# Float32r parts instead of bfloat16 parts for the one-hot gathering and spreading of a mixture-of-experts kernel

## The reference

```python
def hier_moe(x, w_group, w_expert, w_gate, w_up, w_down):
    ...
    rows = xpad[row_tok].reshape(n_blocks, MOE_BLOCK, d)

    def expert_block(args):
        xb, e = args
        h = jax.nn.silu(xb @ w_gate[e]) * (xb @ w_up[e])
        return h @ w_down[e]

    yb = lax.map(expert_block, (rows, block_expert)).reshape(P, d)
    out = jax.ops.segment_sum(yb * row_w[:, None], row_tok, num_segments=T + 1)[:T]
    return out.reshape(b, s, d)
```

## Time and profile before

| | |
|---|---|
| median of 3 runs | 1808.4 us (1807.47 to 1808.51) |
| profiled execution, span | 1806.1 us |
| PE busy | 1786.0 us (99%) |
| DVE, ACT, POOL busy | 721.9, 448.2, 70.9 us |
| moved by DMA | 527.41 MB, of it 516.70 MB through SP's queue |
| float32 gate and up products, L876 | 1856 recorded |
| gathering in bfloat16, L810 | 672 recorded, 78.0 us |
| spreading in bfloat16, L928 | 270 recorded, 69.4 us |

### The profile page before, as it was taken

How to read it: one execution, slowest core, us unless ns; L and a number is a source line. 1 busy time by engine, 2 the same in 40 slices (tenths; PEclk the granted TensorE clock), 3 DMA queues, 4 the chain that set the end, 5 groups by cost and what they waited for, 6 DMA issues and landing times.

```text
span 1806.1 us, 21261 instructions
## 1 busy us (share of the span) xinstructions
PE 1786.0 (99%) x8612; PEld 984.0 (54%) x8647; DVE 721.9 (40%) x1667; ACT 448.2 (25%) x958; POOL 70.9 (4%) x66
## 2 busy tenths in 40 slices
PE   9999999999999999999999999999999999999999
PEld 8888754443443333455444344343366767568874
DVE  3566754212221213035421221221345566234675
ACT  2332312111111100133210111110134534217780
POOL 0000000000000000000000000000011110001110
PEclk9999999999999999999999999999999999999999
DMA  9723569999999999708899999999942332041520
GB/s 389 305 83 139 193 254 410 420 427 428 426 428 429 427 427 425 309 1 349 357 425 428 428 427 427 428 427 427 425 162 94 140 123 110 7 181 47 236 91 23
DMA packets 41828, 527.41 MB, mean 292 GB/s; under 512 B 4800, under 2 KB 5472, under 8 KB 8576
## 3 DMA queue, kind: packets, MB, share of 16 engines
q1 hardware_dynamic: 39200, 516.70, 68.7%
q10 hardware_dynamic: 2528, 9.31, 1.3%
HBM read 524.91 MB, written 1.08 MB: 291 GB/s over the span
## 4 chain that ended last, share of the span: by engine, by line
PE 88%; DMA 9%; DVE 2%; SPq 1%; ACT 0%; issue 0%; POOL 0%; DVEq 0%; ACTq 0%
PE ps L212 32%; PE ps L876 20%; PE ps L911 10%; DMA ring<-in_wu 6%; PE ps L810 4%; PE ps L928 3%; PE ps L715 2%; DMA ring<-in_w_lat 2%; PE ps L1702 2%; PE ps L1670 2%; PE ps L1234 1%; PE ps L679 1%; PE ps L1717 1%; PE ps L883 1%; PE ps L1446 1%; PE ps L1459 1%
## 5 line engine op out<-in xcount | busy, mean ns | idle before, releaser
L876 PE MATMUL ps<-ring,work 128*64 128x512 f32 x1856 | 409.1, 593 | 6.0 <-DMA ring<-in_wu 5.7
L212 PE MATMUL ps<-xl,ring 128*128 128x256 f32 (+3 forms) x1344 | 291.5, 375 | 0.4 <-DMA ring<-in_w_x 0.4
L876 PEld LDWEIGHTS ps<-ring,work 128*64 128x64 f32 x1856 | 131.6, 137 | 270.7 <-issue 251.2
L212 PEld LDWEIGHTS ps<-xl,ring 128*128 128x128 f32 x1344 | 243.7, 190 | 39.5 <-issue 2.5
L911 PE MATMUL ps<-ring,work 128*64 128x512 f32 x816 | 181.5, 594 | 0.1
L212 PE MATMUL ps<-ring,xl 128*128 128x256 f32 (+1 forms) x576 | 176.0, 463 | 0.2 <-ACT xl L1787 0.2
L2647 DVE TENSOR_TENSOR work<-work,ps 128x512 f32<-128x512 f32 x32 | 22.0, 688 | 361.4 <-PE ps L876 341.7
L212 PEld LDWEIGHTS ps<-ring,xl 128*128 128x128 f32 x576 | 108.3, 190 | 59.3 <-issue 49.9
L911 PEld LDWEIGHTS ps<-ring,work 128*64 128x64 f32 x816 | 56.2, 137 | 100.3 <-issue 98.7
L3178 POOL TENSOR_TENSOR small<-small,halves 128x1 f32<-128x1 f32 (+4 forms) x42 | 45.7, 1087 | 1545.7 <-DVE small L2449 936.6
L2608 DVE SCALAR_TENSOR_TENSOR work<-ps,small,big 128x512 f32<-128x512 f32 x60 | 45.0, 750 | 135.8 <-ACT big L1918 135.8
(11 more groups left out here) (476 smaller groups left out, 1958.9 us busy)
## 6 DMA issues: line engine op xcount, KB each, us to landing
ring<-in_wg SPq DMA_DIRECT2D x62, 2048.0 KB, 20.6
ring<-in_wu SPq DMA_DIRECT2D x52, 2048.0 KB, 21.7
ring<-in_wd SPq DMA_DIRECT2D x48, 2048.0 KB, 22.0
xl<-in_wd SPq DMA_DIRECT2D x10, 2048.0 KB, 23.5
xl<-in_wu SPq DMA_DIRECT2D x9, 2048.0 KB, 19.1
ring<-in_w_odd SPq DMA_DIRECT2D x8, 2048.0 KB, 7.4
ring<-in_w_xz SPq DMA_DIRECT2D x7, 2048.0 KB, 22.9
ring<-in_w_qkv SPq DMA_DIRECT2D x6, 2048.0 KB, 34.3
```

Source lines behind the costliest of these rows:

```text
L212: i = e.matmul(bout, lhs(k), rhs(k), start=start and k == ks[0], stop=stop and k == ks[-1])
L876: last = e.matmul(b[64 * j:64 * j + 64, :], x[:, 4 * a + k, 64 * j:64 * j + 64], w[k // 2][:, 2 * (k % 2) + j, :], start=a + k == 0, stop= ...
```

## The change

The 0/1 matrices, the parts of h and the parts of the result rows are kept as float32r, another four-byte type of the language, and a value is split into two such parts, not three. So

- a gathering is 16 products of 256 columns, not 24, and a spreading 8 of 512 columns, not 12;
- DVE makes one further part of each half of the result rows, not two, and the parts of h are one copy (ACT) and one subtraction (DVE) a layer;
- the slot product is 2 products for all 128 rows, not 4 for 64 each, and its table loses the third part of the weights;
- the parts of the result rows, `yr`, take 1 MB, and it is the 1 MB of `lnb` (`yr` is named at the same place as `lnb`, `hr` at that of `big`, the matrices at that of `work`).

So `lnb` is no longer free during the mixture. `BESIDE` is gone: chunk `md` of pair 8 is loaded whole through the ring, and ACT's DMA is no longer there. The norm's parameters can be loaded only once the spreading of pair 14 has read `yr`, so SP waits for that.

```diff
-BESIDE, TAIL = (8, 0), (15, 1)
+TAIL = (15, 1)
...
+        with nc.sbuf_tensor("yr", [128, 2, 1024], F32R) as yr:
+            pass
         lnb = sb("lnb", [128, 2, 1024])
+        with nc.sbuf_tensor("hr", [128, 2, 2, 1024], F32R) as hr:
+            pass
         big = sb("big", [128, 16 * 272])
+        with nc.sbuf_tensor("sr", [128, 2, 2, 256], F32R) as sr, nc.sbuf_tensor("swt", [128, 2, 256], F32R) as swt, \
+                nc.sbuf_tensor("tab", [128, 2, 32, 4], F32R) as tab:
+            pass
...
                         o, c = b[:, k * 256:(k + 1) * 256], (4 * (s % 2) + 2 * i + k) * 128
-                        for t, j in each(range(2), range(3)):
-                            last = e.matmul(o, hb[:, j, t, c:c + 128], Sb[:, s // 2 % 2, t, :],
-                                            start=t + j == 0, stop=t + j == 3)
+                        for t, j in each(range(2), range(2)):
+                            last = e.matmul(o, hr[:, j, t, c:c + 128], sr[:, s // 2 % 2, t, :],
+                                            start=t + j == 0, stop=t + j == 2)
...
-                if (p, n) == BESIDE:
-                    blocks[0:2] = [beside[:, 0:1024], beside[:, 1024:2048]]
-                    landed = {0: (ln_in, 16 * (3 * l + 2)), 2: landed[0]}
-                elif (p, n) == TAIL:
+                if (p, n) == TAIL:
...
-                for j in range(3):
-                    last = e.matmul(macc[t][n][:, :], SWT[:, p % 2, t * 128:(t + 1) * 128], ypart(j, n),
+                for j in range(2):
+                    last = e.matmul(macc[t][n][:, :], swt[:, p % 2, t * 128:(t + 1) * 128], yr[:, j, n * 512:(n + 1) * 512],
                                     start=p + j == 0, stop=False)
...
             e.activation(s4[:, :, 4], s4[:, :, 3], ACT.Exp).then_inc(*e_exp.up(l))
-            e.wait_ge(*ln_out(f"m{l}", 1, 1))
-            e.dma_start(beside, A["wd"][l, BESIDE[0], BESIDE[1]][:, 0:2048]).then_inc(ln_in, 16)
...
-            if n:
-                e.wait_ge(*ys0(l, p))
-            e.scalar_tensor_tensor(out=hs, in0=row_b[n][:, :], scalar=wsl[:, p % 2:p % 2 + 1], in1=ypart(0, n),
-                                   op0=ALU.mult, op1=ALU.subtract).then_inc(*vs.up())
-            e.wait_ge(*vs())
-            e.tensor_copy(ypart(1, n), hs).then_inc(*vs.up())
-            e.wait_ge(*vs())
-            e.tensor_tensor(ypart(2, n), hs, ypart(1, n), ALU.subtract).then_inc(*(ys1 if n else ys0).up(l, p))
+            part = slice(n * 512, (n + 1) * 512)
+            e.scalar_tensor_tensor(out=yr[:, 1, part], in0=row_b[n][:, :], scalar=wsl[:, p % 2:p % 2 + 1],
+                                   in1=yr[:, 0, part].bitcast(F32), op0=ALU.mult, op1=ALU.subtract
+                                   ).then_inc(*(ys1 if n else ys0).up(l, p))
...
-                        elif name == "md" and (p, a) == BESIDE:
-                            e.wait_ge(*ring.before(name, l, p, a))
-                            sync_part(e, w[l, p, a], slice(2048, 4096), ring(name, l, p, a)[0], name, l, p, a)
...
-            e.wait_ge(*dn_mm(l, *BESIDE))
+            e.wait_ge(*spr_mm(l, NE // 2 - 2))
             load_ln(e, 2 * l + 1)
```

More of the change, by code:

```diff
@@ L12 @@
 F32 = mybir.dt.float32
+F32R = mybir.dt.float32r
 BF16 = mybir.dt.bfloat16
@@ L470, in build, with rows_of @@
         m = Arena(work, 7680)
[L471 to L478, removed]
+        m(1792)
+        token, scaled = m(128).bitcast(BF16), m(128)
         xgT, sg, hs, hT = m(2, 8, 256), m(512), m(512), m(4, 128)
         xR = xgT[:, 1]
[L481 to L482 removed]
+        ys = area(big, 0, (1024,))
         mst = small[:, 696:700]
[L484 to L489, removed]
         aside = [big[:, 2048:4096], xgT[:, 1].rearrange("p k n -> p (k n)")]
[L492 removed]
+        def rows_of(s, t):
+            return sr[:, s // 2 % 2, t, 128 * (s % 2):128 * (s % 2) + 128]
         gx, hx, hTx = area(big, 2048, (512,)), area(big, 2560, (512,)), area(big, 3072, (4, 128))
@@ L819, in tensor_slots @@
                 e.wait_ge(*swt_in(l, 0))
-            for j, t in each(range(2), range(2)):
-                o, c = ps[0][64 * j:64 * j + 64, 0:4], 128 * (p % 2) + 64 * j
-                if p < 2:
-                    last = e.matmul(o, S[:, p, t, 64 * j:64 * j + 64], tabf[:, t, 2 * p + j, :], start=t == 0, stop=t == 1)
-                else:
-                    last = e.matmul(o, Sb[:, p // 2 % 2, t, c:c + 64], tab[:, t, 2 * p + j, :], start=t == 0, stop=t == 1)
+            for t in range(2):
+                last = e.matmul(ps[0][:, 0:8], rows_of(p, t), tab[:, t, 2 * p:2 * p + 2, :].rearrange("p e c -> p (e c)"),
+                                start=t == 0, stop=t == 1)
             last.then_inc(*slot_mm.up(l, p))
@@ L2591, in vector_slots @@
             i = p % 2
-            e.tensor_copy(slot[:, i], ps[0][:, 0:4]).then_inc(*vs.up())
+            for j in range(2):
+                r = slice(64 * j, 64 * j + 64)
+                e.tensor_copy(slot[r, i], ps[0][r, 4 * j:4 * j + 4]).then_inc(*vs.up())
             e.wait_ge(*vs())
-            e.tensor_reduce(wsl[:, i:i + 1], slot[:, i, 1:4], AXX, ALU.add).then_inc(*vs.up())
-            e.tensor_scalar(SWTf if p == NE // 2 - 1 else SWT[:, i], token, slot[:, i, 0:1], None, ALU.is_equal
+            e.tensor_reduce(wsl[:, i:i + 1], slot[:, i, 1:3], AXX, ALU.add).then_inc(*vs.up())
+            e.tensor_scalar(swt[:, i], token, slot[:, i, 0:1], None, ALU.is_equal
                             ).then_inc(*swt_in.up(l, p))
```

46 lines of the change are left out of this document (16 added, 30 removed).

## The result

| | median of its runs | lowest to highest |
|---|---|---|
| kernel before, beside the changed one | 1807.7 us (10 runs) | 1806.4 to 1808.5 |
| changed kernel | 1812.3 us (10 runs) | 1811.0 to 1813.4 |

The ratio is 1.0025, 95% interval 1.0016 to 1.0035: the changed kernel is 4.5 us slower. The forecast was +4.9 us, 1813.3. The profiled execution has a span of 1810.5 us, against 1806.1.

The account below looks back on a forecast made before the run. The prediction took the full DMA engines, through the landing of each mixture's last chunks, to bound the kernel. Its terms, +4.9 for the half chunk and four zeros, on 1808.4 gave 1813.3 us, range 1808 to 1820.

Parts of the forecast that it names:

- The bound: In the mixtures the DMA engines are full; 29.5 us a pair against PE's 26.57, so the last chunks' landing sets the end.
- Part 1: Pair 8's half chunk moves from a DMA hole into the full stretch: 1.049 MB, 2.46 us a layer, +4.9 us.
- landing isn't held back: Rival, chance 0.11: 427 GB/s throughout the stretch gives back 0.8 us a layer, 1811.7; no change from about 1.4.
- Part 2: PE in the mixture's middle: cheaper float32r products save 24.9 us a layer, but PE only waits for the landing, so nothing.
- The lower end: Gathering and spreading: float32r products cost the same as bfloat16, 0.212 and 0.109 us, a gain of 1.72 us a pair.
- the transposes' row: Four float32 transposes in 0.44 us, 0.11 for 128 columns, the nearest evidence for float32r products of 0.43 and 0.216 us.
- the middle price: Rival, chance 0.07: float32r products at 0.43 and 0.216 us, PE loses 25.3 us a layer, +43, 1852.
- the bound from the weight load: Gathering: float32 weight loads of 190 ns make sixteen products at least 3.04 us; without overlap a rival, +75, 1883, chance 0.03.
- Part 3: Behind the last up chunk: less spreading, but the path goes through DVE and ACT; 0, at most 0.4 us a layer.
- Part 4: SP's wait for pair 14's spreading before the norm's parameters: nothing, covered by 4 us of DMA work left.
- the sum: Five terms over the whole kernel: +4.9 + 0 + 0 + 0 + 0 on 1808.4, giving 1813.3 us.
- The signs: Profile after: first weight wait near 505 us, DMA at 427 GB/s, empty hole, layer 0's last up chunk at 697 us.

Follow-up runs that it names:

- kernel before with the lighter load: Kernel before, one half of every second chunk of pairs 3 to 14 not loaded in both layers (results wrong): 1797.8 us, ratio 0.9941.
- two kernels with the lighter load: Kernel before and changed kernel, each without one half of every second chunk of pairs 3 to 14 (results wrong): 1797.8 and 1761.0 us.

## Why the prediction was right, point by point

**The bound.** Right. The end of a mixture is the landing of its last up chunk, by four runs: the half chunk alone costs what the change costs, leaving it out gives 4.0 us back, three give 14.5, and 9 us lost by PE in the middle give and take nothing.

**Part 1, the half chunk, +2.46 a layer.** The mechanism was right, and the size too high in the changed kernel: 1.57 and 2.03 us, 3.6 for the two, not 4.9. For the half chunk by itself it was nearly right: the kernel before with this edit alone lost 1.95 and 2.68, 4.6 for the two, and one half chunk less in the changed kernel gained 2.94 in layer 0. Differences of up to 0.6 us in one landing say nothing. What part 1 left out is that with float32r parts the DMA engines' rate answers a little. Packets and MB from 280 to 690 us, before and then after:

```profile
DMA packets 12354, 174.74 MB, mean 426 GB/s; under 512 B 1367, under 2 KB 1367, under 8 KB 1367
```

```profile
DMA packets 12297, 175.03 MB, mean 427 GB/s; under 512 B 1357, under 2 KB 1357, under 8 KB 1357
```

The changed kernel moved 0.29 MB more in the same time, 0.7 us of work. The other kernels bear it out: 174.93 to 175.04 MB in the four more with float32r and no half chunk in the hole, 174.79 in the two more with bfloat16 parts. It was made up early: from 300 to 350 us the rate is 422 GB/s, before 418. This is the rival "landing isn't held back" at half its strength: it had to give back 1.4 us a layer to count. The hole before 280 us stayed nearly empty, as forecast (70 GB/s from 276 to 280 us, where the kernel before moves 276).

**Part 2, float32r.** The lower end was the right choice, but not exact. Its price of a bfloat16 spreading was misread: the chain has eleven of the twelve products, and the missing one is the "issue" piece ahead of them. The kernel before with the lighter load has all twelve:

```profile
476.81 0.16 issue
```

```profile
477.12 2.69 PE ps L928 x12
```

So a spreading took 2.70 us, 0.225 a product, not 2.54 and 0.212; the pair's 26.57 us hold it already. The float32r products cost 0.256 and 0.119 us, not 0.212 and 0.109. A pair falls by 26.57 - 25.26 = 1.31 us, not 1.72: 0.65 in the spreading, 0.71 in the gathering, the rest in the slot and down products. That is 18.4 us a layer by the two kernels with the lighter load, not 24.9. That the transposes' row does not stand for float32r was a choice, given as one with its chance, and it held: the middle price, 0.43 and 0.216, is out. So is the bound from the weight load: it is 190 ns in float32r, as feared, yet sixteen of them with their products take 1.91 us and not 3.04. The page's group of these loads has 55.1 us for 448, 0.123 each, so they overlap each other in the record, and here the mean of a weight load is no floor for the distance of products. Apart from the rate above, none of this reached the time, since all of it lies behind the transfers, as the prediction said.

**Part 3, nothing gained behind the last up chunk.** Right: from there to the down product it takes 702.05 - 696.21 = 5.84 us, before 700.47 - 694.64 = 5.83.

**Part 4, the new wait.** Right at nothing, ratio 1.0 in the run with it alone, but for a wrong reason. I said that the DMA engines have 4 us of work left when SP is released and don't run dry. They do run short: in the changed kernel they move 332 GB/s from 700 to 702 us and 270 from 702 to 704, where the kernel before moves 424 and 412, which is 1.1 us of work. It costs nothing because what comes late is not waited for: the parameters' load is issued at 701.87 us in layer 0, and the one in layer 1 lands 6.6 us after its issue. By that it is there at about 708.5, an estimate, and DVE wanted it at 710.56 even before.

**What the sum did not have.** The gap of 1.28 us behind the branch, +1.56 in the timeline and 0.9 to 1.8 by the times of the two kernels that have it not, and the wait of 0.60 us for the next stage's weights in layer 1, which was a wait of PE for something that doesn't move with PE's own lateness and went when PE came later. With part 1 too high by 1.3 us, the errors cancel: 3.6 + 1.56 - 0.7 = 4.5, against 4.9. That the total came nearer than its terms is luck; the bound and its price in bytes are not. The new gap is a part of the changed kernel's loss that has nothing to do with its idea: with it moved away, the changed kernel is at 1810.4 to 1810.6, still 3 us above the kernel before.

**The signs.** Of those I had named, the row x448, DMA at 427 to 428, the empty hole, and the last up chunk near 697 (696.21) came. The first wait for weights in layer 0 stands at 508.70 us and is short (0.38), the first long one (1.33) at 513.68; the forecast said near 505. The waits were 41.1 us in all, not 60, since the products were dearer than I took them to be. PE's busy time fell by 25.3 us, not 50: a pair saves 1.31 us, and the groups that wait are recorded longer.

## What to carry to other kernels

When DMA and PE are both near full, ask which one runs out of lead: a pair's bytes at the measured rate against a pair's PE time tells it before any change, and then only bytes and holes in the transfers count, however much PE work is saved. On-chip space that lets a transfer start in an otherwise empty hole is then worth its bytes over the full rate, and should not be paid for faster products that wait. A gap marked "issue" that comes without any change nearby may belong to the place of the code; move the code by some dozens of instructions before you explain it. Look at the granted clock behind such a gap, and at that of every execution: here executions with a mean clock of 0.999 were 2 to 3 us longer than others of the same kernel, half of what the change costs, where the clock fell at the end of a mixture.

## What the runs showed of the hardware that I had not expected

- A float32r product of 128 x 128 weights takes 0.256 us for 512 columns and 0.119 for 256, with a weight load of 190 ns; in bfloat16 it was 0.225, 0.109 and 98 ns (the first from the kernel before with the lighter load, the others from the earlier trace rows). Two float32r parts are cheaper than three bfloat16 parts, 3.96 us against 5.32 for a pair's gathering and spreading, by less than the count of products says. The Trainium skill, "TensorE: Matmul & The Clock Gate", Weight-path perf modes, keeps the fast weight load from FP32 and doesn't name float32r; the float32r load's 190 ns are those of float32.
- PE can stand still for 1.28 to 3.10 us at one place of its code behind a branch, and 32 instructions more ahead of the place made the gap vanish. 96 waits already met, in one place, went with a stop of 6.34 us.
- The granted clock fell to its lower level, 1.2 GHz, for a while behind some of these stops, those of 1.98, 3.10 and 6.34 us, and not behind those of 3.07, 1.71 and 1.28 us. With 3.10 us it made eight products 1.7 us longer, with 6.34 us 64 products 2.9 us longer.
- The rate of a full stretch is no constant: from 300 to 350 us it was 409 to 425 GB/s in the eleven kernels that keep the transfers full, 427 to 428 from 350 us on.
